# Two layers' weight groups and PSUM banks reordered, and the low parts of four input sums moved from GpSimd to VectorE

## The reference, cut to what matters

```python
# end of the first block
e = (p[i] @ w_ple[i]) * jax.nn.sigmoid(h @ w_ple_gate[i])
h = h + rmsnorm(e, norm_ple_post[i])
# second block
h = rms_norm(x, ffn1_norm[l])
x = x + 0.5 * ((silu(h @ ffn1_w_gate[l]) * (h @ ffn1_w_up[l])) @ ffn1_w_down[l])
h = rms_norm(x, mix_norm[l])
z = h @ w_in[l] + b_in[l]
...
x = x + merged @ w_out[l]
h = rms_norm(x, ffn2_norm[l])
x = x + 0.5 * ((silu(h @ ffn2_w_gate[l]) * (h @ ffn2_w_up[l])) @ ffn2_w_down[l])
```

## Time and profile before

| | us |
|---|---|
| median of 3 runs | 2133.61 (2133.14 to 2134.15) |
| the profiled execution | 2133.07 |
| its span | 2131.3 |
| TensorE (PE) busy | 2104.1 |
| VectorE (DVE) busy | 1097.4 |
| ScalarE (ACT) busy | 990.4 |
| GpSimd (POOL) busy | 980.2 |

### The profile page before, as it was taken

How to read it: one execution, slowest core, us unless ns; L and a number is a source line. 1 busy time by engine, 2 the same in 40 slices (tenths; PEclk the granted TensorE clock), 3 DMA queues, 4 the chain that set the end, 5 groups by cost and what they waited for, 6 DMA issues and landing times. The chain is left out here.

```text
span 2131.3 us, 30936 instructions
## 1 busy us (share of the span) xinstructions
PE 2104.1 (99%) x12144; PEld 1786.6 (84%) x12144; DVE 1097.4 (51%) x2009; ACT 990.4 (46%) x1759; POOL 980.2 (46%) x489
## 2 busy tenths in 40 slices
PE   9999999999999999999999999999999999999998
PEld 8788877787888888888999888778888888999986
DVE  7684555446655500588666123654444126766611
ACT  7835545545544422455545222672346235554521
POOL 4432422345544443646665444034524445766631
PEclk9999999999999999999999999999999999999999
DMA  4212321232322332212333223022331222233321
GB/s 180 98 51 105 119 69 50 106 112 80 106 93 99 110 107 89 89 60 93 112 104 122 86 99 114 21 80 100 109 88 62 99 99 80 100 110 110 119 89 50
DMA packets 56448, 200.79 MB, mean 94 GB/s; under 512 B 6640, under 2 KB 7536, under 8 KB 55920
## 3 DMA queue, kind: packets, MB, share of 16 engines
q1 hardware_dynamic: 52416, 188.77, 25.2%
q10 hardware_dynamic: 3888, 10.05, 1.4%
HBM read 194.60 MB, written 2.10 MB: 92 GB/s over the span
## 5 line engine op out<-in xcount | busy, mean ns | idle before, releaser
L882 POOL TENSOR_TENSOR w_lo<-raw,w_hi 128x1024 fp32r<-128x1024 f32 x281 | 692.5, 2475 | 916.4 <-ACT w_hi L1796 888.5
L1796 ACT ACTIVATE w_hi<-raw 128x1024 fp32r<-128x1024 f32 x284 | 294.9, 1051 | 131.6 <-PE dense L1040 77.7
L824 POOL TENSOR_TENSOR w_lo<-raw,w_hi 128x512 fp32r<-128x512 f32 x102 | 132.9, 1317 | 109.4 <-ACT w_hi L1802 109.4
L1036 PE MATMUL dense<-u_hi,w_hi 128*128 128x512 f32 x432 | 168.8, 391 | 0.0
L1040 PE MATMUL dense<-u_hi,w_lo 128*128 128x512 f32 x432 | 168.1, 389 | 0.0
L1039 PE MATMUL dense<-u_lo,w_hi 128*128 128x512 f32 x408 | 158.7, 389 | 0.0
L2841 DVE SCALAR_TENSOR_TENSOR h<-dense,h 128x512 f32<-128x512 f32 x24 | 16.6, 691 | 200.8 <-PE dense L1040 200.8
L1062 PE MATMUL dense<-s_hi,w_hi 128*128 128x256 f32 x408 | 115.8, 284 | 0.4 <-DVE slot L2822 0.4
L1063 PE MATMUL dense<-s_lo,w_hi 128*128 128x256 f32 x408 | 115.4, 283 | 0.0
L1064 PE MATMUL dense<-s_hi,w_lo 128*128 128x256 f32 x408 | 115.4, 283 | 0.0
L1036 PE MATMUL misc<-u_hi,w_hi 128*128 128x512 f32 x280 | 109.3, 391 | 2.3 <-POOL w_lo L882 2.3
(11 more groups left out here) (586 smaller groups left out, 5772.4 us busy)
## 6 DMA issues: line engine op xcount, KB each, us to landing
raw<-in_weights SPq DMA_DIRECT2D x352, 512.0 KB, 3.2
h<-in_x SPq DMA_DIRECT2D x4, 512.0 KB, 6.9
alibi<-in_alibi ACTq DMA_DIRECT2D x1, 2048.0 KB, 8.1
h<-in_x ACTq DMA_DIRECT2D x2, 1024.0 KB, 7.2
out<-result SPq DMA_DIRECT2D x8, 256.0 KB, 2.2
p_raw<-in_p ACTq DMA_DIRECT2D x2, 512.0 KB, 3.2
hn<-mqk ACTq DMA_DIRECT2D x4, 256.0 KB, 4.0
mqk<-mqk ACTq DMA_DIRECT2D x4, 256.0 KB, 3.4
```

Of the source, the lines that this page charges most:

```text
L824: nc.gpsimd.tensor_tensor(piece(w_lo, p, i), src, piece(w_hi, p, i).bitcast(F32), ALU.subtract).then_inc(st_pool, 1)
L882: nc.gpsimd.tensor_tensor(w_lo[:, ring(s), :, :], raw[:, s % RAWS, :, :], w_hi[:, ring(s), :, :].bitcast(F32), ALU.subtract).then_inc(w_sp ...
L1036: first = mm(out, hi, x_hi, start=(i == 0), stop=False)
L1796: f(w_hi[:, ring(s), :, :], raw[:, s % RAWS, :, :], ACT.Copy).then_inc(w_part, 1)
```

## The change

1. In the weight stream and on TensorE `ple_gate7` comes before `ple7`, and the filler behind them is 7 matmuls, not 10.
2. `down1`'s groups 4 to 7 take the banks 2, 3, 4, 5 (before: 2, 3, 0, 1). `down2` keeps its banks.
3. `out`'s groups take the banks 0, 1, 2, 3, 0, 1, 4, 5 (before: 1, 2, 3, 0, 1, 2, 3, 0).
4. In `up1` ScalarE rounds all slabs up to that of group 11 (slabs 153 and 154 are then added at this place) right behind `sum_hi_of`, before the silu of pair 3. Before, they were rounded in front of the silu of pair 4.
5. In `up2` the four `s_lo` are made by VectorE, behind pair 0's gate and value (`c == 0`), and no longer by GpSimd.

```diff
-    a += [("ple7", 1, 2, 0), ("ple_gate7", 1, 8, 0)]
+    a += [("ple_gate7", 1, 8, 0), ("ple7", 1, 2, 0)]
...
-        for name in PAIRED:
-            for m in range(DC):
-                bank_of[START["down" + name[2:]][1] + m] = (2, 3, 0, 1)[m % 4]
+        for m in range(DC):
+            bank_of[START["down1"][1] + m] = (2, 3, 0, 1, 2, 3, 4, 5)[m]
+            bank_of[START["down2"][1] + m] = (2, 3, 0, 1)[m % 4]
+            bank_of[START["out"][1] + m] = (0, 1, 2, 3, 0, 1, 4, 5)[m]
...
-                if c == PAIRED[name][0]:
-                    for i in SUM_ORDER if name == "up2" else ():
-                        pool.wait_ge(st_hi, sum_no(name, i + 1, BLOCKS))
-                        nc.gpsimd.tensor_tensor(s_lo[i][:, :, :], s_all[:, i, :, :], s_hi[i][:, :, :].bitcast(F32),
-                                                ALU.subtract).then_inc(st_slo, 1)
...
+            dense("ple_gate7", u_hi, ug_lo, row="post2", row_at=(0, DC - 2))
             dense("ple7", p_hi, p_lo)
-            dense("ple_gate7", u_hi, ug_lo, row="post2", row_at=(0, DC - 2))
             pe.wait_ge(ple_sig, 7)
-            stay_busy(10)
+            stay_busy(7)
...
                         for i in range(4):
                             sum_hi_of(name, i)
+                        feed(name, 2 * paired_from - 1)
...
                     if unscaled == paired_from and c == 2:
                         input_sums(name, 2 * DC + 4)
+                    if c == (2 if unscaled == paired_from else 0):
                         for i in SUM_ORDER:
                             dve.wait_ge(st_hi, sum_no(name, i + 1, BLOCKS))
                             TT(s_lo[i][:, :, :], s_all[:, i, :, :], s_hi[i][:, :, :].bitcast(F32),
```

## The result

The changed kernel takes 2138.42 us (median of 15 runs, 2137.50 to 2139.40), the one before 2134.15 in the same session (15 runs, 2133.14 to 2137.52). The ratio is 1.0021, with a 95% interval of 1.0014 to 1.0027: slower by 4.3 us (0.2%), where 1.7 were forecast. The profiled execution has a span of 2135.8 us against 2131.3, which is 4.5 more, so it can be read for the whole loss.

The account below looks back on a forecast made before the run. TensorE, busy 2104.1 of 2131.3 us, was taken as the bound. Against the profiled 2133.07, -0.62 - 0.60 - 1.05 + 1.34 + 2.6 = +1.7; with the median 0.5 above the profile, 2135.3 us, range 2128.5 to 2137.8.

Parts of the forecast that it names:

- The tie at `wq`: After `wq` group 1: `slot_r` ready at 1269.03, its sum matmul due at 1269.07, just holding; -0.60 us (0 to -0.64).
- The rival that the banks save nothing: New banks of `down1` and `out` gain nothing, ties going the other way; sum +3.3, 2136.9 us; chance 0.10.
- the way to the block: `up1`, from `s_lo` to the first paired block: VectorE 4.5 us late, `pair_three` rounded at 975.3, rewriting starts at 978.6.
- the turns rule: VectorE operations with two SBUF inputs and GpSimd ones reading SBUF exclude each other; issue order decides; gives +1.3 in `up1`.
- the step that failed: First paired block of `up1`: TensorE's third product at 985.7, 2.7 us gained at group 10, 4.0 given back; +1.3 us.
- The bound: Upper limit for the early rounding in `up1`: one more turn lost to GpSimd in `u_lo`, +2.5 us.
- the row where VectorE kept its turn: GpSimd's operation at 982.53 took 2.05 us, not 1.30, letting a later-issued VectorE one pass; would give -0.7 in `up1`.
- the slower rival: New waits at the first blocks of `up1` and `up2` lower TensorE's clock, 1.8 us each; +5.3, 2138.9 us; chance 0.08.
- Gains kept: VectorE's lateness in `up1` stays hidden and both work moves gain, -3.5 and -0.5; sum -6.3, 2127.3 us; chance 0.15.
- half of it: VectorE keeps its turns: -0.7 in `up1`, +0.5 in `up2`; sum -2.5, 2131.1 us; chance 0.22.

Follow-up runs that it names:

- keep_clock: Changed kernel plus 14 filler matmuls on TensorE in the wait ahead of `up1`'s first paired block; 2137.77 us, ratio 1.0014.
- hold_low: Changed kernel, with GpSimd's last low part of `up1`'s first paired block waiting until all eight `u_lo` are made; 2135.63 us, ratio 1.0008.
- both_held: Changed kernel, GpSimd's last low part in `up1`'s first block held behind all `u_lo`, its `three` in `up2`'s behind the four rounded sums; 2133.53 us.
- three_held: Changed kernel, with GpSimd's `three` of `up2`'s first paired block waiting until ScalarE has rounded the four sums; 2136.87 us, ratio 1.0016.
- three_again: Same program as three_held, nothing changed, one more profiled execution; 2137.70 us.
- keep_again: Same program as keep_clock, nothing changed, one more profiled execution; 2138.78 us.
- late_hold: Kernel before plus changes 1 to 4; GpSimd's slab 153 low part held behind `s_lo`, its last in `up1`'s first block behind `u_lo`; 2129.34 us.
- late_low: Kernel before plus changes 1 to 4, with GpSimd taking slab 153's low part only behind the fourth `s_lo`; 2132.62 us, ratio 0.9992.
- only_feed: Kernel before with only change 4, slabs 153 and 154 of `up1` rounded before the silu of pair 3; 2137.68 us, ratio 1.0017.
- orders_banks: Kernel before with only changes 1 to 3: `ple_gate7` first with 7 fillers, new banks of `down1` and `out`; 2132.21 us, ratio 0.9992.
- only_slo: Kernel before with only change 5, `s_lo` of `up2` made by VectorE behind pair 0; 2137.18 us, ratio 1.0016.

## Why the prediction was wrong

- **Parts 1 to 3** right: -0.54, -0.46 and -1.02 against -0.62, -0.60 and -1.05. The tie at `wq` cost 0.14 of part 2: `slot_r` is ready at 1272.64, and the sum matmul starts at 1272.79. The rival that the banks save nothing is refuted.
- **Part 4**, the way to the block: right in kind. The last two `s_lo` take 3.43 and 3.41 us, the `a_lo` behind them 2.88. `pair_three` is rounded at 974.88 (forecast 975.3), the rewriting starts at 978.04 (978.6). The third product is +1.94 from the start of the layer, where +1.3 was put; 0.4 of that is the lower clock (keep_clock, at the full clock, has +1.50). This is the turns rule at work. The Trainium skill ("SBUF — State Buffer", "Who interferes with whom") has issue order decide; in `s_lo` the trace agrees: GpSimd starts at 958.00 and the third `s_lo` at 958.06, and GpSimd goes first.
- **Part 4, the size: the step that failed.** "That comes at 985.7. TensorE has gained 2.7 us at group 10 and gives back 4.0: +1.3 us" ends the walk at the third product. The fourth waits for VectorE's first output, behind `u_lo` 7, `u_lo` 8 and `a_lo`, and three turns are lost there. It measured +4.24. The bound had "one more turn lost in `u_lo`, +2.5": one turn, at about the right price, where three were lost, since behind GpSimd's low part `three` and the next block's first low part stood ready, and each of these took a turn as well. With GpSimd held there, the part is +1.0 (hold_low), +0.9 (both_held).
- **Part 5** right: +2.42 against +2.6, and by the order worked out. Less the +2.10 with which `up2` starts, the copy of the first product comes at 1820.0 (1822.14) and the third product at 1820.5 (1822.63), where the forecast had 1820.2 and 1820.7. `pair_one` still loses one turn, as forecast.
- **The rule against the row.** The forecast weighed "issue order decides" against the row where VectorE kept its turn, and took the rule. It left out that in the same profile `a_lo` lost a turn right behind it. Both happen, in one program: in the profiles of three_held and keep_clock VectorE keeps its turns beside the very operation to which it loses them in three_again and keep_again. By the starts in the profile GpSimd is first at each turn that VectorE loses in the long ones (984.50 against 984.71 in three_again), as the rule has it; but it is first in the quick ones too (983.75 against 983.96 in three_held) and there goes last. So these traces don't bear out that the order of start alone settles it. An execution in which VectorE keeps them would be 3.3 us less than 2138.4, near the forecast; none of the fifteen was one by its time, while two in eleven of three_held and five in eleven of keep_clock were.
- **The clock**: the slower rival had it fall behind waits longer than the 2.7 us seen before, at 1.8 us each, where in the runs such a stretch cost 0.6 to 1.0. It does fall, behind the wait of 3.35, but does not hold up the fourth product: hold_low with a fall and keep_clock without have it at +1.49 and +1.50 from the start of `up1`. In `up2` it does not fall in the changed kernel. That this rival's time, 2138.9, is near the measured one is luck.
- **Gains kept and half of it**: the changed kernel shows neither. Part 4 gains (-2.0) only in late_hold, with GpSimd held at both places. With the turns lost in `s_lo` and kept behind it, it is +0.9 to +1.0.

What stays open: what decides, from one execution to the next, who gets the turn. Between keep_clock and keep_again no start on VectorE, ScalarE or GpSimd from 968 us up to the contest differs by more than 0.02 us, counted from GpSimd's low part, and no kernel here moved the low part by a part of an operation to see. Nor is it shown why the changed kernel loses the turns in all fifteen runs, as their times say.

## What to carry over

When work is moved onto or next to an engine that loses turns to another, follow the queue not to the first late consumer but until nothing behind it is later than before, and count every operation that the other engine has ready: each is a turn of its own. A wait that keeps the neighbour out of the critical run cost nothing here, where its work wasn't due, and the second group of times went with the lost turns (both_held, late_hold). Look at all the single times before reading one profile: two groups mean that a profile shows one of two courses.

## What the runs showed of the hardware

- A VectorE operation with both inputs in SBUF and a GpSimd one beside it: 1.77 us instead of 0.68 at 512 columns when it loses its turn to one of about the same size, 3.4 instead of 1.22 at 1024. GpSimd's low part of 512 columns takes 1.30 alone, 1.44 when it goes first, and 3.26 when VectorE keeps three turns (three_held). Which it is can differ between executions of one program, 3.3 us apart in time here.
- Before the last 15 us of the kernel, the granted clock of TensorE was half for 3.4 us at a time (once 6.8) in nine of thirteen profiles, but not in those of before, keep_clock, late_low and late_hold. All six profiles with a wait of 3.30 to 3.36 us ahead of the block (changed, only_feed, hold_low, both_held, three_held, three_again) have a fall there, between 1.1 us before the wait's end and 1.8 us behind it. At the wait before group 10 it fell in orders_banks (2.38 us) and only_slo (2.51), and not in before (2.31). Such a stretch in which TensorE had work to do cost 0.6 to 1.0 us (orders_banks, only_slo, hold_low). In hold_low, with the wait of 2.46 us in `up2`, the offset goes from +1.70 to +2.56 across the stretch behind it:

```profile
1820.40:1823.80 3.40, 3.40 (x18) 3.40 (x18) 1.77 (x3) 2.51 (x5) 3.40 (x3) 0.50 0.41 148
1823.80:1830.00 6.20, 6.18 (x51) 6.01 (x51) 4.46 (x10) 2.66 (x5) 3.80 (x4) 1.00 0.31 91
```

The changed kernel and keep_clock have the same wait there, 2.48 and 2.49 us long, and no fall: a wait of this length doesn't decide it alone.
